# Small transfers moved from SyncE's queue to GpSimd's, and two parts of the gated units at later steps

## The reference

```
first:   h = rms_norm(x);  x = x + (silu(h @ w_ffn_gate) * (h @ w_ffn_up)) @ w_ffn_down
second:  val, gate = split(h @ w_up)
         gate[t] = b + w[0]*gate[t-2] + w[1]*gate[t-1] + w[2]*gate[t]      (per channel)
         x = x + (val * gelu(gate)) @ w_down
```

## Time and profile before

| | |
|---|---|
| Median of 3 runs | 2873.36 us |
| Profiled execution | 2874.23 us |
| Its span, first to last instruction | 2873.0 us |
| PE busy | 2853.3 us (99%) |
| DVE busy | 1657.3 us (58%) |
| ACT busy | 1313.6 us (46%) |
| POOL busy | 183.6 us (6%) |
| Granted clock of PE | 0.999 |

### The profile page before, as it was taken

One profiled execution on the slowest core, in us unless ns is written; L12 is line 12 of the kernel. 1 busy time (PEld: TensorE's weight loads), 2 busy tenths in 40 slices (PEclk: granted clock), 3 DMA queues, 4 the chain that ended last, 5 costly groups with the idle time before them and its releaser, 6 DMA issues.

```text
span 2873.0 us, 32355 instructions
## 1 busy us (share of the span) xinstructions
PE 2853.3 (99%) x13256; PEld 2348.4 (82%) x13256; DVE 1657.3 (58%) x1788; ACT 1313.6 (46%) x1592; POOL 183.6 (6%) x221
## 2 busy tenths in 40 slices
PE   9999999999999999999999999999999999999998
PEld 7878887788888888888878888887888888878887
DVE  5464555555555555555585457655756676666444
ACT  5444445444445444444454455444544444444443
POOL 0000000000000000000000029900100000000000
PEclk9999999999999999999999999999999999999999
DMA  7555454456555566666765556554667788787563
GB/s 258 197 164 193 158 190 152 164 191 202 183 190 184 186 209 216 183 224 206 206 204 184 190 172 194 170 181 152 199 203 243 238 254 256 232 262 238 188 204 133
DMA packets 385115, 571.34 MB, mean 199 GB/s; under 512 B 114821, under 2 KB 117649, under 8 KB 384966
## 3 DMA queue, kind: packets, MB, share of 16 engines
q1 hardware_dynamic: 363264, 540.07, 58.0%
q10 hardware_dynamic: 21702, 29.18, 3.4%
HBM read 544.09 MB, written 2.10 MB: 190 GB/s over the span
## 4 chain that ended last, share of the span: by engine, by line
PE 84%; DVE 7%; SPq 3%; DMA 3%; ACT 1%; issue 1%; ACTq 1%; POOL 0%; DVEq 0%
PE panels L634 27%; PE panels L636 27%; PE panels L635 27%; DVE weights_lo L1830 3%; SPq L390 3%; DMA gate_shifted<-ffn_gate 2%; PE side L658 2%; ACT weights_hi L1233 1%; DMA hiddenT_lo<-ffn_gate 1%; DVE ffn_hidden L1995 1%; DVE ffn_gate L2001 0%; DVE ffn_gate L2029 0%; DVE ffn_gate L2032 0%; ACTq L1396 0%; DVE ffn_gate L2031 0%
## 5 line engine op out<-in xcount | busy, mean ns | idle before, releaser
L1830 DVE TENSOR_TENSOR weights_lo<-weights,weights_hi 128x1024 fp32r<-128x1024 f32 (+1 forms) x1032 | 1247.9, 1217 | 1079.9 <-ACT weights_hi L1233 1075.7
L1233 ACT ACTIVATE weights_hi<-weights 128x1024 fp32r<-128x1024 f32 (+1 forms) x1032 | 1062.9, 1036 | 1220.7 <-PE panels L636 1175.2
L634 PE MATMUL panels<-weights_hi,xT_hi 128*128 128x512 f32 (+1 forms) x2748 | 1076.3, 392 | 4.6 <-DVE weights_lo L1830 4.3
L636 PE MATMUL panels<-weights_hi,xT_lo 128*128 128x512 f32 (+1 forms) x2752 | 1068.2, 388 | 0.0
L635 PE MATMUL panels<-weights_lo,xT_hi 128*128 128x512 f32 (+1 forms) x2752 | 1068.1, 388 | 0.0
L634 PEld LDWEIGHTS panels<-weights_hi,xT_hi 128*128 128x128 f32 x2748 | 516.1, 188 | 121.7 <-DVE weights_lo L1830 10.8
L636 PEld LDWEIGHTS panels<-weights_hi,xT_lo 128*128 128x128 f32 x2752 | 516.7, 188 | 107.3
L635 PEld LDWEIGHTS panels<-weights_lo,xT_hi 128*128 128x128 f32 x2752 | 517.1, 188 | 103.6 <-issue 0.2
L634 PE MATMUL panels<-weights_hi,hiddenT_hi 128*128 128x512 f32 x704 | 275.0, 391 | 0.2 <-DVE weights_lo L1830 0.2
L636 PE MATMUL panels<-weights_hi,hiddenT_lo 128*128 128x512 f32 x704 | 274.0, 389 | 0.0
L635 PE MATMUL panels<-weights_lo,hiddenT_hi 128*128 128x512 f32 x704 | 273.9, 389 | 0.0
(11 more groups left out here) (355 smaller groups left out, 1849.3 us busy)
## 6 DMA issues: line engine op xcount, KB each, us to landing
weights<-in_w_in SPq DMA_DIRECT2D x162, 1024.0 KB, 5.0
weights<-in_w_up SPq DMA_DIRECT2D x88, 1024.0 KB, 7.3
weights<-in_w_ffn_gate SPq DMA_DIRECT2D x44, 1024.0 KB, 5.2
weights<-in_w_ffn_up SPq DMA_DIRECT2D x44, 1024.0 KB, 5.5
weights<-in_w_out SPq DMA_DIRECT2D x32, 1024.0 KB, 5.2
weights<-in_w_ffn_down SPq DMA_DIRECT2D x32, 1024.0 KB, 5.1
weights<-in_w_down SPq DMA_DIRECT2D x32, 1024.0 KB, 5.2
weights<-in_w_ffn_down SPq DMA_DIRECT2D x16, 768.0 KB, 4.6
```

What stands on the lines that cost most here:

```text
L634: pe.matmul(acc, a, wh, start=k0 + k == 0, stop=False)
L636: inst = pe.matmul(acc, b, wh, start=False, stop=k0 + k == total - 1)
L1233: self.act.activation(self.m.HI[:, g % PIECES, 0:n], raw, ACT.Copy).then_inc(self.ev["hi_split"])
L1830: self.dve.tensor_tensor(m.LO[:, ring, 0:n], raw, m.HI[:, ring, 0:n].bitcast(F32), ALU.subtract).then_inc(self.ev["lo_split"])
```

## The change

The sixteen transfers of each unit are issued by POOL instead of SP. POOL's program has the eleven units' moves of the first network behind the norm before it, and those of the second behind the fifth norm; each unit's moves wait for its transposition as before. SP's program is then weights loads alone.

In the first network the high part of a hidden block goes from step 7 of the next gate panel to the third step of the up panel behind it, the low part one step later. In the second network both go to the up panel too, as a work beside gelu (ACT) and beside the convolution (DVE). Gelu is one step later. The last unit's high and low parts in the down panels are three and four steps later in one network, and three in the other.

```diff
(Sync.program)
-            if c in blocks_in:
-                self.move_blocks(blocks_in[c])
...
(Pool.program)
         self.half_power(2, m.RSTD)
+        for n in range(FF // PANEL):
+            self.move_blocks(n)
         self.half_power(3, m.RX)
...
         self.half_power(5, m.RSTD)
+        for n in range(FF // PANEL):
+            self.move_blocks(FF // PANEL + n)
         self.half_power(6, m.RSTD)
+
+    def move_blocks(self, n):
+        self.pool.wait_ge(self.ev["hidden_blocks"], n + 1)
...
+                self.pool.dma_start(dst[:, i], blocks[32 * i:32 * i + 32, j]).then_inc(self.ev["loaded_hidden_in"], 16)
(Scalar)
-                 together(self.hidden_high(3), self.ssm_setup()))
+                 together(self.hidden_high(6), self.ssm_setup()))
...
-        side.add(self.norm_rows(plan.ffn2[-1], t["final_norm_g_2"]), self.hidden_high(3))
+        side.add(self.norm_rows(plan.ffn2[-1], t["final_norm_g_2"]), self.hidden_high(6))
...
-            if i:
-                side.add(self.hidden_high(6))
+            if i and not second:
+                side.add(self.hidden_high(10))
...
-                side.add(self.gelu(i, panels))
+                side.add(together(*([self.hidden_high(2)] if i else []), self.gelu(i, panels)))
...
-        for _ in range(6):
+        for _ in range(7):
             yield
         act.wait_ge(ev["convolved"], i + 1)
(Vector)
-        side.add(self.pause(2), together(self.hidden_low(4), self.ssm_setup()))
+        side.add(self.pause(2), together(self.hidden_low(8), self.ssm_setup()))
...
-        side.add(self.hidden_low(7))
+        side.add(self.hidden_low(10))
...
-            if i:
-                side.add(self.hidden_low(7))
+            if i and not second:
+                side.add(self.hidden_low(11))
...
-                side.add(self.conv2(i))
+                side.add(together(*([self.hidden_low(3)] if i else []), self.conv2(i)))
```

More of the change, by code:

```diff
@@ L363, in program @@
         sp.dma_start(m.X[:, :, 3 * PANEL:D], x[:, :, 3 * PANEL:D]).then_inc(ev["loaded_x_load4"], 16)
-        pairs = self.plan.ffn1 + self.plan.ffn2
-        blocks_in = {up.chunk0 + 9: n for n, (_, up) in enumerate(pairs)}
         for c, (pan, k0, nk) in enumerate(self.plan.chunks):
@@ L380, in program @@
         sp.wait_ge(ev["loaded_stores"], 16 * 5)
[L382 to L390, removed]
     def load_chunk(self, c, pan, k0, nk):
@@ L421, in program @@
         self.half_power(5, m.RSTD)
+        for n in range(FF // PANEL):
+            self.move_blocks(FF // PANEL + n)
         self.half_power(6, m.RSTD)
+    def move_blocks(self, n):
+        self.pool.wait_ge(self.ev["hidden_blocks"], n + 1)
+        blocks = self.m.BLOCKS.rearrange("p (c j q) -> p j c q", j=4, q=32)
+        at = n % (FF // PANEL) * (PANEL // P)
+        for j in range(4):
+            dst = self.m.HL[32 * j:32 * j + 32, at:at + 4, :].bitcast(F32).rearrange(
+                "r k (t i q) -> r i (k t) q", t=TT, i=4)
+            for i in range(4):
+                self.pool.dma_start(dst[:, i], blocks[32 * i:32 * i + 32, j]).then_inc(self.ev["loaded_hidden_in"], 16)
     def step(self, inst):
```

## The result

| | before | after |
|---|---|---|
| median of the runs, us | 2873.52 (2871.96 to 2874.25, 4 runs) | 3043.76 (3040.08 to 3045.29, 4 runs) |
| profiled execution, us | 2874.2 | 3042.56 |
| span, us | 2873.0 | 3041.3 |

The change makes the kernel slower by 5.9%: the ratio is 1.0592, with an interval of 1.0578 to 1.0606. The forecast was 2894.5 us in a range of 2863 to 2932; the time lies 112 us above its upper end.

The account below looks back on a forecast made before the run. PE bounds the kernel, with at most 8.5 us to save. The second network's loop of 27.1 + 19.7 = 46.8 us, against PE's 43.52, loses 29.7 instead of 8.5: +21.2, so 2894.5 us, range 2863 to 2932.

Parts of the forecast that it names:

- what POOL takes for one move: Moves on POOL: 0.67 us of queue work plus 0.47 per instruction, 1.14 each; 19.7 us for a unit's moves.
- The first part: Second network's loop, gate read to end of transposition: 27.1 us in place of 28.4.
- rival B: POOL's moves hold each other up, three under way: 1.9 us a move, about 3100 us; 0.15 together with D.
- Rival D: VectorE and GpSimd hinder each other, so what stands beside a POOL instruction can stretch it; 0.15 together with B.
- the milder price: Rival B's lower price for POOL's moves: 1.35 us a move, a time of 2928 us.
- Rival A: POOL's transfers take at most 0.96 us, PE's pace takes over: 2865 us, up to 2868; chance 0.28.
- The steps: New ACT and DVE order, second network: first convolution product 12.1 us after the gate read, transposition end at 27.1.
- gelu's wait: ACT's wait before gelu in the second network, cut to near 2 to 3 us a unit.
- its cover: First network: ACT can be 4.6 us late at no loss; gone if sixteen moves exceed 23.6 us, then 10 × the excess.

Follow-up runs that it names:

- three_on_pool: Changed kernel with the moves back in SyncE's queue, except the first three of each unit's 16, issued by GpSimd: 2866.07 us, ratio 0.9972 to the kernel before.
- sp_waits: Changed kernel, but SyncE loads no further weights from a set chunk on until the unit's 16 moves have landed: 2974.37 us, ratio 1.0345 to the kernel before.
- sems4: Changed kernel with the moves counted on four semaphores in turn instead of one: 2964.16 us, ratio 1.0312 to the kernel before.

## Why the prediction was wrong

**The step that failed: what POOL takes for one move.** The prediction bounded it "not below SP's 0.67 us" and took 1.14. The issue is 0.58, below the bound, and the mean with the standings is 1.7 in the unit shown, above the value. The moves of the second network took 26.3 to 28.9 us from the transposition to the next gate read, 27.5 on average, not 19.7. The first part was 26.9 on average, so this one term holds all of the excess of a unit: 26.9 + 27.5 = 54.4 us. A smaller term of it was off too: POOL starts 0.5 us after the transposition in the unit shown, not 0.1.

The failure was one of kind. The price was built of work for each instruction, 0.67 of a queue plus POOL's 0.47, as if any number of moves could be under way. Where only so many fit (the queue's depth, here three), the price of a move is (issue of a group + standing) / group, and a standing is the landing of the group's last move and 0.35 us: (1.74 + 1.6) / 3 = 1.11 us with no weights beside it, and (1.74 + 5) / 3 = 2.2 with them. The first value is near the (1.14 + 2.5) / 3 = 1.2 of rival B at the median landing, and by chance nearly the 1.14 that I took for another reason.

**Rival B was the mechanism**: POOL's moves hold each other up, since no more than three are under way and three cost one issue and one landing. That three fit was a supposition of mine, which no row of the kernel before shows; the groups of three at 1024 bytes in the section on the result do. With D it had 0.15, too small a chance. Its price was an estimate: 1.14 us for the issue and a landing of 4.6, the middle of 2.5 and 6.8, 5.7 / 3 = 1.9 us a move all through; the milder price was 1.35, with a time of 2928. The 1.9 was somewhat high: in every unit of the second network the last standing is 1.6 us, free of weights. Its loop of 59 us was 54.4, and the time of about 3100 became 3044. Against it I had the median landing of 2.5 us. That median was of SP's queue, where sixteen go out in 10.70 us without a gap, while earlier ones are landing, and where only the last landing is waited for, 1.3 us behind the last issue. With room for three every group pays it. The line also showed a maximum of 6.8, and the DMA share of 0.77 in the earlier trace rows spoke for it.

**Rival A** was right on the issue (0.58 is under its 0.96) and wrong on the time. The moves would have been done in 9.3 us without the standing. **Rival D** is out: the 352 issues of the changed kernel have a median of 582 ns and a maximum of 758, beside a DVE busy 55% of the span, and `three_on_pool` loses no time. Nor does DVE make the standings: in `sp_waits` 79 of 112 last 1.5 to 1.7 us, with DVE busy for anything from 0 to 95% of a group's time.

**The steps were right.** The first convolution step (L2025) at 12.1 us (12.1 to 12.2 in units 2 to 11), transposition end at 27.0 (27.1), gelu's wait 2.6 us in the unit shown ("near 2 to 3"), gate read put down to the moves' landing. The forecast for the first part of the loop held within 0.1 us while everything else moved.

**The first network.** The prediction named the point at which its cover goes: 23.6 us for the moves, and ten times the excess beyond. Measured from transposition to gate read: 25.3 to 28.5 us, mean 27.1, so 3.5 us a unit. A unit lost 49.15 − 43.52 = 5.6. Of the other 2.1 us, some 1.6 are a thing that was in no sum, the clock. The trace has a record of half clock (0.50), 3.4 to 13.7 us long, at the end of each of PE's 19 stops of 3 us or more, or within 1.3 us behind it. It makes the gate and up panels longer: from gate read to transposition 21.8 us on average in the first network against 20.2 in `sems4`, where PE stops for less and no record of half clock is found in that stretch. The changed kernel's own units say the same: the two of units 2 to 11 that have no half clock in that stretch take 20.2 us, the eight that have it 21.8 to 23.0. Granted clock of the changed kernel around one such place, instructions on `panels`:

```profile
1012.00:1020.00 8.00, 4.07 (x18) 3.06 (x17) 0.00 (x0) 1.27 (x2) 1.00 0.06 12
1020.00:1024.00 4.00, 4.00 (x13) 3.14 (x12) 0.00 (x0) 0.00 (x0) 0.57 0.90 287
1024.00:1040.00 16.00, 16.00 (x72) 13.23 (x71) 1.41 (x2) 0.00 (x0) 1.00 0.58 196
```

PE stood for half of the first eight microseconds, waiting for the late gate read; 13 matmuls fit in the next four where 18 would at full clock. From 1021 to 1023 the granted clock is 0.50 and a matmul starts every 0.43 us, not every 0.23; from 1024 on it is 1.00 again. In the second network the loop is bound elsewhere, and the first part took 27.0 us with the clock at 0.93 as without: I find no cost of the half clock there.

## What to carry to other kernels

GpSimd's queue had a price for issuing, 0.58 us, and a depth, three moves at 1024 bytes of scratch, and a step that issued sixteen in a row paid the issue of three and their landing for each filling; ask for the depth before the issue. Take the landing that the transfers will have beside their neighbours (up to 6.3 us here), not its median in another queue (2.5). Look at how they are counted: on one semaphore the room came back by the group, on four move by move. Where a buffer is given back only when the last of many small transfers has landed, issue them from the queue that takes them all without a pause, here SyncE's with sixteen in 10.70 us: the new steps alone, with the moves left on SyncE, gave 2865.67 us, 0.29% under the kernel before.

## What the runs showed of the hardware

GpSimd issued these transfers at 0.58 us each, quicker than SyncE's 0.67. It stood after two, three, five or six of them as the scratch was 640, 1024, 1408 or 1856 bytes, for 1.6 us with no weights beside it whatever the size of the group, and for 2.6 to 5.9 in the units shown with them. Counted on one semaphore, it went on 0.35 us after the last of the group had landed (110 of 111 standings of the changed kernel); on four, with room for three, 0.31 us after the landing of the transfer three before (157 of 160 in `sems4`), which took 80 us off the kernel. Their packets did not run in the 2.8 us in which SyncE's loads kept the engines 91% busy.
